# DeltaNet: the second half's inverse of the diagonal squares on GpSimd instead of VectorE

## The chip, the cores and the metric

The kernel runs on one core of a Trainium2 chip. A core has a matrix engine (PE, TensorE), a vector engine (DVE, VectorE), a scalar engine (ACT, ScalarE), a general engine (POOL, GpSimd) and a queue engine (SP, SyncE) that here only issues transfers. Each engine takes its own instructions in the order in which they were written and they meet through semaphores. ACT also issues transfers (rows "ACTq"): while it issues one it does nothing else.

The metric is the device time of one execution in microseconds (us). A profiled execution has a time of its own; all rows below are from it.

## The reference, cut to what matters

One layer of a hybrid encoder over 1024 tokens: four mixers feed a gated merge, then come cross attention and a mixture of experts. The change concerns the mixer called gated DeltaNet, run forward and backward over the sequence. Its core is one unit lower-triangular system for each chunk, head and direction:

```python
kk = jnp.einsum('bhntd,bhnsd->bhnts', kc, kc)
a_mat = jnp.where(strict, bc[..., None] * kk * decay, 0.0) + jnp.eye(c)
rhs = jnp.concatenate([vc * bc[..., None], kc * (bc * jnp.exp(gam))[..., None]], axis=-1)
sol = lax.linalg.triangular_solve(a_mat, rhs, left_side=True, lower=True, unit_diagonal=True)
u_val, k_cum = sol[..., :dv], sol[..., dv:]
# then chunk after chunk:
v_new = u_i - kc_i @ state
o = qd_i @ state + qk_i @ v_new
state = cd_i * state + kd_i^T @ v_new
```

## The kernel before, in words

**One list of steps.** `plan_schedule` writes one list of steps for all engines; each engine walks it and emits what it has to do for each step, so the list fixes the order on every engine. `dense(...)` lays out the matrix products of the weight panels (PE line L794) in parts; a `None` in the list given as `between` takes the next part (6 matmuls for most) and a named step stands between the parts. So PE works through panels, and the mixer's small products stand between their parts.

**DeltaNet in tiles.** The sequence is cut into TT = 8 tiles of 128 tokens; tile step i handles tile i forward and tile 7-i backward, for 4 heads: 8 matrices of 128x128 in each step. `gdn_a` (i = 0 to 7) builds the matrices and writes them to HBM (`gdn_out`), and ACT copies their 32x32 diagonal squares into `GDIAG` (L1728). After tile 3 and after tile 7 the squares of four tiles go to HBM (`gdn_ship`, L1767; halves b = 0 and 1), and `gdn_read` (L1777) brings them back so that each of the 128 partitions holds one square of 32x32 in `NUT[b]` and `NU[b]`.

**The inverse.** `gdn_inv(b, first, next)` inverts the 128 squares of half b at once, column by column: for j = 1 to 30 a product of a column with a row into a scratch tile (L2407) and a subtraction from the rows below (L2410), each of (31-j)*j elements in a partition and each waiting for the one ahead. A copy of half the partitions, turned, stands in front (L2402); two passes over 1024 elements (L2413, L2415) and two memsets (L2418) stand at the end. All of it is on DVE, in ten pieces of three columns that stand between other steps: those of half 0 from tile 5 of `gdn_a` on, those of half 1 within tiles 0 to 2 of `gdn_c`.

**Back and out.** `gdn_back(b)` (ACT, L1783) writes the inverses to HBM, `gdn_load_inv(i)` (ACT, L1803) loads those of one tile step into `XZC`, and `gdn_c(i, part)` with parts 0 to 6 solves and advances the state. In part 0 POOL spreads the squares into block-diagonal matrices `NX` and `NZ_` (L2825, four instructions in a step), which PE waits for with its first small product of the tile (L1015). In part 1 POOL makes two scaled copies of k for each direction (L2843, L2845). Half 1's inverses are first wanted for tile 4.

## Time and profile before

| what | us |
|---|---|
| median of 3 runs | 2041.04 (2040.8 to 2041.76) |
| the profiled execution | 2028.88 |
| its span | 2027.1 |
| PE busy in the span | 1878.2 (93%) |
| DVE busy | 1384.4 (68%) |
| ACT busy | 1078.0 (53%) |
| POOL busy | 308.8 (15%) |
| DeltaNet's `gdn_a` and both inverses, roughly | 668 to 844 |
| tile steps 0 to 7 of `gdn_c` | 773 to 945 |

Busy shares are means over stages that differ. What counts for the change is who waits for whom between 740 and 860 us, and what each engine does there. The profiled execution is 12.2 us shorter than the median of the timed runs.

### The profile page before, as it was taken

To read this page: it belongs to the slowest core of one execution; us is meant where nothing else is said; L and a number is where in the kernel's file an instruction comes from. 1 tells how busy PE (TensorE), PEld (TensorE's weight loads), DVE (VectorE), ACT (ScalarE), POOL (GpSimd) and SP (SyncE) were. 2 spreads that over 40 slices of the span, in tenths; PEclk is the share of its full clock that TensorE was granted. 3 is DMA by queue.
4 is the path that set the end of the run, shared out by engine and by line. 5 is a ranking of instruction groups with operands and counts; after the bars stand their busy time and mean duration, and the time that the engine had idled before them with its cause. 6 is when DMAs were issued, how large, how long until landed. Compare 5 with 4: busy or idle time off the path is not lost.

```text
span 2027.1 us, 32760 instructions
## 1 busy us (share of the span) xinstructions
PE 1878.2 (93%) x12949; PEld 1117.6 (55%) x12949; DVE 1384.4 (68%) x1833; ACT 1078.0 (53%) x1568; POOL 308.8 (15%) x269
## 2 busy tenths in 40 slices
PE   6999999999999989899999999995899999999991
PEld 3464565655544545677488755684455444444440
DVE  5555533799974797544733745437799999999997
ACT  4573223566646541223433533334588888888873
POOL 5000100344310512231000000000000111111103
PEclk9999999999999999999999999997899999999996
DMA  5411111212011562441522510404799999999986
GB/s 193 159 52 43 32 42 48 73 48 58 22 28 47 194 201 79 142 122 45 213 65 67 157 32 16 169 32 161 279 422 422 422 422 422 422 422 423 422 346 269
DMA packets 145817, 366.80 MB, mean 181 GB/s; under 512 B 39296, under 2 KB 94880, under 8 KB 119072
## 3 DMA queue, kind: packets, MB, share of 16 engines
q1 hardware_dynamic: 96608, 279.57, 36.3%
q10 hardware_dynamic: 40240, 52.50, 7.7%
q0 software_dynamic: 8848, 33.03, 4.2%
q8 instruction: 86, 1.41, 0.3%
q14 instruction: 35, 0.29, 0.0%
HBM read 314.14 MB, written 46.73 MB: 178 GB/s over the span
## 4 chain that ended last, share of the span: by engine, by line
PE 77%; DVE 10%; ACT 5%; issue 4%; DMA 2%; ACTq 1%; SPq 1%; DVEq 0%; POOLq 0%
PE psum L794 39%; PE psum L1185 24%; ACT arena L1631 2%; PE psum L1174 1%; PE psum L1109 1%; PE psum L1084 1%; DVE arena L2308 1%; PE psum L924 1%; PE psum L1203 1%; PE psum L811 1%; DMA gdn_lq<-arena 1%; PE psum L1066 1%; PE psum L1044 1%; DMA arena<-in_w_in_dram 1%; PE psum L935 1%
## 5 line engine op out<-in xcount | busy, mean ns | idle before, releaser
L794 PE MATMUL psum<-arena 128*128 128x512 f16 (+2 forms) x6000 | 1013.4, 326 | 17.6 <-ACT arena L1375 6.8
L794 PEld LDWEIGHTS psum<-arena 128*128 128x128 f16 x6000 | 567.6, 98 | 398.6 <-issue 15.6
L1185 PE MATMUL psum<-arena 128*128 128x512 f16 x2304 | 512.3, 381 | 14.7 <-issue 11.7
L751 DVE SCALAR_TENSOR_TENSOR arena<-arena 128x2048 f16<-128x2048 f32 x192 | 437.3, 2286 | 58.0 <-ACT arena L745 57.8
L745 ACT ACTIVATE arena<-arena 128x2048 f16<-128x2048 f32 x192 | 365.3, 1908 | 72.4 <-DMA arena<-in_w_dram 43.2
L1185 PEld LDWEIGHTS psum<-arena 128*128 128x128 f16 x2304 | 224.5, 98 | 280.4 <-issue 22.1
L1965 DVE SCALAR_TENSOR_TENSOR arena<-arena 128x512 f16<-128x512 f32 (+1 forms) x185 | 125.8, 699 | 114.0 <-ACT arena L1349 113.5
L2862 POOL DMA_INDIRECT arena<-xhat,arena x32 | 66.2, 2069 | 839.8 <-PE psum L1174 445.2
L1349 ACT ACTIVATE arena<-arena 128x512 f16<-128x512 f32 (+1 forms) x212 | 127.2, 616 | 51.5 <-issue 19.9
L1375 ACT ACTIVATE arena<-psum,arena 128x512 f32<-128x512 f32 x60 | 41.0, 684 | 140.3 <-PE psum L794 139.6
L1438 ACT ACTIVATE arena<-psum 128x512 f32<-128x512 f32 (+3 forms) x51 | 29.9, 586 | 126.4 <-PE psum L794 126.4
L1403 ACT ACTIVATE arena<-arena 128x256 f32<-128x256 f32 x64 | 26.7, 416 | 109.7 <-DVE arena L2000 108.6
L2757 POOL TENSOR_SCALAR arena<-arena 128x512 f32<-128x512 f32 x27 | 57.5, 2130 | 138.3 <-ACT arena L1349 138.3
L2293 DVE CUSTOM_DVE_ANT_0 arena<-psum,arena 128x1024 f32<-128x1024 f32 x64 | 75.6, 1219 | 2.3 <-PE psum L911 2.2
L1631 ACT ACTIVATE arena<-arena 128x1024 f32<-128x1024 f32 x64 | 72.9, 1147 | 7.3 <-DVE arena L2293 7.2
L1988 DVE SCALAR_TENSOR_TENSOR arena<-arena,psum 128x512 f32<-128x512 f32 x64 | 43.8, 684 | 42.7 <-PE psum L794 31.9
L2000 DVE SCALAR_TENSOR_TENSOR arena<-psum,arena 128x512 f32<-128x512 f32 x32 | 22.1, 690 | 65.1 <-PE psum L794 65.1
L2018 DVE SCALAR_TENSOR_TENSOR arena<-psum,arena 128x512 f16<-128x512 f32 x36 | 24.8, 690 | 59.9 <-ACT arena L1438 31.0
L1640 ACT ACTIVATE arena<-psum 128x512 f16<-128x512 f32 x64 | 34.7, 594 | 55.1 <-PE psum L924 34.3
L2825 POOL TENSOR_TENSOR arena<-arena 128x512 f32<-128x512 f32 x32 | 34.5, 1109 | 144.5 <-PE psum L1052 92.4
L1880 ACT ACTIVATE arena<-psum 128x512 f32<-128x512 f32 x64 | 38.2, 597 | 13.9 <-PE psum L1185 13.1
L1174 PE MATMUL psum<-arena 128*128 128x128 f32 x256 | 34.5, 279 | 8.8 <-DMA arena<-xhat,arena 8.8
(388 smaller groups left out, 2017.4 us busy)
## 6 DMA issues: line engine op xcount, KB each, us to landing
arena<-in_w_dram SPq DMA_DIRECT2D x192, 1024.0 KB, 11.9
arena<-in_merge_w_dram SPq DMA_DIRECT2D x64, 256.0 KB, 3.2
yrows<-arena ACTq DMA_DIRECT2D x32, 512.0 KB, 7.8
arena<-in_w_in_dram SPq DMA_DIRECT2D x48, 256.0 KB, 2.8
gdn_lq<-arena ACTq DMA_DIRECT2D x8, 1024.0 KB, 4.5
arena<-gdn_lq ACTq DMA_DIRECT2D x8, 1024.0 KB, 5.0
arena<-in_xattn_wkv_dram SPq DMA_DIRECT2D x32, 256.0 KB, 3.0
yrows<-arena POOLq DMA_DIRECT2D x1, 7680.0 KB, 24.1
```

What stands on the lines that cost most here:

```text
L745: nc.scalar.activation(half_of(pieces(e, m)[0], half), half_of(XLAND[m], half), ACT.Copy, scale=WS).then_inc(w_hi[m], 1)
L751: nc.vector.scalar_tensor_tensor(half_of(lo, half), half_of(XLAND[m], half), WS, half_of(hi, half), ALU.mult, ALU.subtract).then_inc(w_lo[ ...
L794: mm = nc.tensor.matmul(bank[prt[0]:prt[1], c0:c1], lhs[a](k), rhs[b](k), start=(k == 0 and a + b == 0), stop=(k == nk - 1 and a == 1))
L1174: tr = nc.tensor.transpose(PS[:, k // 4, (k % 4) * P:(k % 4) * P + P], xs[:, k, :], ident)
L1185: mm = nc.tensor.matmul(PS[:, bank, :], left[a][:, k, :], right[b][:, k, columns], start=k + a + b == 0, stop=(k == n - 1 and a == 1))
L1349: S.activation(W[i % 2][0][:, 2 * j:2 * j + 2, 0:wide], LAND[c % NLAND][:, :, 0:wide], ACT.Copy, scale=WS).then_inc(*act_hi.mark(c))
L1631: S.activation(DS[u % 2][:, m, :], DS[u % 2][:, m, :], ACT.Exp, scale=-1.0, bias=d_mx[u % 2][:, m:m + 1], accum_out=d_l[u % 2][:, m:m + 1])\
L1965: V.scalar_tensor_tensor(W[i % 2][1][:, 2 * j:2 * j + 2, 0:wide], LAND[c % NLAND][:, :, 0:wide], WS, W[i % 2][0][:, 2 * j:2 * j + 2, 0:wid ...
L1988: V.scalar_tensor_tensor(dst, gate, 1.0, bank, ALU.add, ALU.mult).then_inc(*e.mark(n))
L2293: V.tensor_tensor_reduce(out=DS[u % 2][:, m, :], in0=PS[:, 2 + 2 * m:4 + 2 * m, :].rearrange("p a b -> p (a b)"), in1=DWH[:, 896 - P * qt: ...
L2757: G.tensor_scalar(landed_c, landed_c, WS, None, ALU.mult).then_inc(*counter("pool_w_scaled").mark(chunk))
L2862: G.indirect_dma_start(XR[e % 2], None, XH_D, bass.IndirectOffsetOnAxis(IDX[:, e:e + 1], 0)).then_inc(rows_in[e % 2], 16)
```

## The change

Half 1's inverse moves from DVE to POOL as one step of all 30 columns. It stands in the list right behind piece 6 of half 0's inverse (columns 19 to 21), with `gdn_read(1)` ahead of it, which stood behind the two `gdn_load_inv` before. The scratch tile is `NX[0]` instead of `n_tmp`. `gdn_back(1)` moves from tile 3 to tile 1 of `gdn_c` and waits for POOL.

```diff
     for p in range(5, 10):
         gdn += inv(0, p) + [None] * (2 + (p < 8)) + [("gdn_load", p - 5)] * (p < 7)
-    gdn += [("gdn_back", 0)] + [None] * 6 + [("gdn_load_inv", 0), ("gdn_load_inv", 1), ("gdn_read", 1)] + [None] * 7
+        gdn += [("gdn_read", 1), ("gdn_inv", 1, 1, 31)] * (p == 6)
+    gdn += [("gdn_back", 0)] + [None] * 6 + [("gdn_load_inv", 0), ("gdn_load_inv", 1)] + [None] * 7
     for i in range(TT):
         for part in range(7):
-            gdn += [("gdn_back", 1)] * ((i, part) == (3, 1))
+            gdn += [("gdn_back", 1)] * ((i, part) == (1, 3))
             gdn += [("gdn_c", i, part)] + [None] * (1 + (i < 3 and part in (1, 4) and (i, part) != (2, 1)))
-            if i < 3 and part in (1, 2, 4) or (i, part) == (0, 5):
-                gdn += inv(1, 3 * i + (i > 0) + (1, 2, 4, 5).index(part))
...
-                    act.wait_ge(*counter("vec_gdn").at("inv", b))
+                    act.wait_ge(*counter("pool_gdn" if b else "vec_gdn").at("inv", b))
...
-                elif what == "gdn_inv":
+                elif what == "gdn_inv" and not step[1]:
...
+                elif what == "gdn_inv" and step[1]:
+                    b, first_row, next_row = step[1:]
+                    po = counter("pool_gdn")
+                    U, UT = NU[b], NUT[b]
+                    if first_row == 1:
+                        pool.wait_ge(diag_in[b], 32)
+                        pool.wait_ge(*counter("act_gdn").at("dt", TT - 1, 1))
+                        G.tensor_copy(U[0:64], UT[0:64].rearrange("p r c -> p c r")).then_inc(*po.mark("forward", b))
+                        pool.wait_ge(*po.last())
+                    for j in range(first_row, next_row):
+                        n = 31 - j
+                        part = NX[0].rearrange("p h n -> p (h n)")[:, 0:n * j].rearrange("p (r c) -> p r c", c=j)
+                        G.tensor_tensor(part, bc(U[:, j + 1:32, j:j + 1], P, n, j), bc(U[:, j:j + 1, 0:j], P, n, j), ALU.mult)\
+                            .then_inc(*po.mark("term", b, j))
+                        pool.wait_ge(*po.last())
+                        G.tensor_tensor(U[:, j + 1:32, 0:j], U[:, j + 1:32, 0:j], part, ALU.subtract).then_inc(*po.mark("row", b, j))
+                        pool.wait_ge(*po.last())
+                    if next_row == 31:
+                        G.tensor_scalar(UT, U.rearrange("p r c -> p c r"), -1.0, None, ALU.mult).then_inc(*po.mark("turned", b))
+                        pool.wait_ge(*po.last())
+                        G.tensor_scalar(U, U, -1.0, None, ALU.mult).then_inc(*po.mark("negative", b))
+                        pool.wait_ge(*po.last())
+                        for m in (U, UT):
+                            G.memset(m.rearrange("p r c -> p (r c)")[:, ::33], 1.0).then_inc(*po.mark(*(("inv", b) if m is UT else ("one", b))))
```

POOL before, from its last instruction of `gdn_a` (AFFINE_SELECT) to the first of `gdn_c` tile 0 (L2825, the spread):

```order
L2813 TENSOR_TENSOR arena<-arena 128x512
L2816 AFFINE_SELECT arena<-arena 128x512
L2825 TENSOR_TENSOR arena<-arena 128x512 x4
L2843 TENSOR_TENSOR arena<-arena 128x256
L2845 TENSOR_TENSOR arena<-arena 128x256
```

POOL after, at the end of the inverse and the start of `gdn_c` tile 0 (the spread is now L2848):

```order
L2829 TENSOR_TENSOR arena<-arena 128x30
L2832 TENSOR_TENSOR arena<-arena 128x30
L2835 TENSOR_SCALAR arena<-arena 128x1024
L2837 TENSOR_SCALAR arena<-arena 128x1024
L2840 MEMSET arena 128x32 x2
L2848 TENSOR_TENSOR arena<-arena 128x512 x4
L2866 TENSOR_TENSOR arena<-arena 128x256
```

The whole inverse, 65 instructions in all, stands on POOL ahead of tile 0's spread. ACT before, from the second load of `gdn_lq` to the read of half 1's squares (L1777):

```order
L1793 DMA arena<-gdn_lq 128x2048
L1375 ACTIVATE arena<-psum,arena 128x512
L1349 ACTIVATE arena<-arena 128x512 x2
L1375 ACTIVATE arena<-psum,arena 128x512
L1783 DMA gdn_inv<-arena 128x1024 x2
L1375 ACTIVATE arena<-psum,arena 128x512
L1803 DMA arena<-gdn_inv 128x4x32 x8
L1777 DMA arena<-gdn_diag 64x1024 x2
```

ACT after, the same place (the read is now L1776, the evacuation of a gate L1374):

```order
L1792 DMA arena<-gdn_lq 128x2048
L1776 DMA arena<-gdn_diag 64x1024 x2
L1374 ACTIVATE arena<-psum,arena 128x512
L1348 ACTIVATE arena<-arena 128x512 x2
L1374 ACTIVATE arena<-psum,arena 128x512
L1782 DMA gdn_inv<-arena 128x1024 x2
L1374 ACTIVATE arena<-psum,arena 128x512
L1802 DMA arena<-gdn_inv 128x4x32 x8
```

The read moved ahead of two evacuations and of `gdn_back(0)`. On DVE the 65 instructions of half 1's inverse are gone; PE's order is the same as before.

## Rows read from the trace of the kernel before

**Rows 1.** The page's part 1: busy us (share of the span) xinstructions.
```profile
PE 1878.2 (93%) x12949; PEld 1117.6 (55%) x12949; DVE 1384.4 (68%) x1833; ACT 1078.0 (53%) x1568; POOL 308.8 (15%) x269
```

**Rows 2.** Timeline of PE: start, us, engine line, operands xcount [idle before <-releaser].
```profile
745.28 28.67 PE L794 MATMUL psum<-arena 128*128 128x512 f16 x126 [6.14 <-DVE arena L1988]
776.30 2.76 PE L794 MATMUL psum<-arena 128*128 128x512 f16 x12 [2.35 <-ACT arena L1375]
778.99 0.60 PE L1015 MATMUL psum<-arena 32*32 32x32 f32 x32
...
804.50 0.34 PE L1024 MATMUL psum<-arena 32*32 32x32 f32 x5 [0.95 <-DVE arena L2428]
```

**Rows 3.** Waits of PE between 740 and 880 us: us in total, times, longest.
```profile
PE psum L1038 <- ACT arena L1751: 5.2, 3, 2.2
```

**Rows 4.** Timeline of POOL around the start of `gdn_c`.
```profile
720.42 0.63 POOL L2816 TENSOR_SCALAR_AFFINE_SELECT arena<-arena 128x512 f32<-128x512 f32 x1
773.20 4.48 POOL L2825 TENSOR_TENSOR arena<-arena 128x512 f32<-128x512 f32 x4 [52.15 <-DMA arena<-gdn_inv]
```

**Rows 5.** Timeline of ACT; ACTq rows are transfers that it issues.
```profile
742.75 0.38 ACTq L1767 DMA_DIRECT2D gdn_diag<-arena  x1
...
748.11 0.33 ACTq L1793 DMA_DIRECT2D arena<-gdn_lq  x1
...
763.93 0.82 ACTq L1783 DMA_DIRECT2D gdn_inv<-arena  x2
...
768.65 5.07 ACTq L1803 DMA_DIRECT2D arena<-gdn_inv  x8
773.83 1.10 ACTq L1777 DMA_DIRECT2D arena<-gdn_diag  x2
```

**Rows 6.** DVE, 600 to 1050 us, by line (both inverses): xcount | busy, mean ns.
```profile
L2410 DVE TENSOR_TENSOR arena<-arena 128x30 f32<-128x30 f32 (+14 forms) x60 | 19.9, 332 | 2.1
L2407 DVE TENSOR_TENSOR arena<-arena 128x30 f32<-128x30 f32 (+14 forms) x60 | 19.8, 330 | 1.6
```

**Rows 7.** Timeline of DVE: the end of half 0's inverse.
```profile
763.82 0.09 DVE L2418 MEMSET arena<- 128x32 f32 x1
```

**Rows 8.** Timeline of POOL: what its instructions take at several sizes.
```profile
38.10 1.49 POOL L2757 TENSOR_SCALAR arena<-arena 128x512 f32<-128x512 f32 x1 [3.72 <-ACT arena L1349]
122.39 2.35 POOL L2778 TENSOR_TENSOR arena<-arena 128x1024 f32<-128x1024 f32 x1 [13.13 <-ACT arena L1534]
257.28 1.27 POOL L2783 TENSOR_TENSOR arena<-arena 128x512 f32<-128x512 f32 x1 [2.10 <-DVE arena L2222]
668.50 1.04 POOL L2813 TENSOR_TENSOR arena<-arena 128x512 f32<-128x512 f32 x1 [80.58 <-DMA arena<-gdn_rows]
669.69 0.89 POOL L2816 TENSOR_SCALAR_AFFINE_SELECT arena<-arena 128x512 f32<-128x512 f32 x1 [0.15 <-POOL arena L2813]
...
847.89 0.61 POOL L2843 TENSOR_TENSOR arena<-arena 128x256 f32<-128x256 f32 x1 [0.67 <-DVE arena L2451]
864.80 4.03 POOL L2825 TENSOR_TENSOR arena<-arena 128x512 f32<-128x512 f32 x4 [13.96 <-PE psum L1052]
```

**Rows 9.** Timelines of POOL and DVE: the same operations beside each other and alone.
```profile
700.61 1.47 POOL L2813 TENSOR_TENSOR arena<-arena 128x512 f32<-128x512 f32 x1
...
700.07 1.11 DVE L2387 TENSOR_TENSOR arena<-arena 128x512 f32<-128x512 f32 x1
...
727.42 0.68 DVE L2387 TENSOR_TENSOR arena<-arena 128x512 f32<-128x512 f32 x1
```

**Rows 10.** DMA issues, 690 to 870 us: xcount, KB each, median us to landing.
```profile
gdn_diag<-arena ACTq DMA_DIRECT2D x2, 512.0 KB, 6.6
...
arena<-gdn_diag ACTq DMA_DIRECT2D x4, 256.0 KB, 5.0
```

**Rows 11.** Stretches of 2 us: length, busy (x) of PE, PEld, DVE, ACT, POOL, then PEclk.
```profile
746.00:748.00 2.00, 2.00 (x6) 0.76 (x5) 1.90 (x5) 0.00 (x0) 0.00 (x0) 0.51 1.43 206
748.00:750.00 2.00, 2.00 (x11) 0.88 (x9) 1.90 (x5) 0.63 (x1) 0.00 (x0) 1.00 1.13 242
```

## The prediction, made before the changed kernel was run

> **What bounds the kernel now.** First the shares: PE is busy for 93% of the span, DVE for 68%, POOL for 15% [rows 1]. That says that PE's waits are what costs, not DVE's load, but it is a mean. So next comes the timeline of PE from 740 us on, where DeltaNet's second stage begins. From 745.28 PE runs 126 panel matmuls without a gap, waits 2.35 us for ACT's evacuation of a gate, runs 12 more, and at 778.99 takes the first small product of tile 0 (L1015) [rows 2]. Behind that it waits little: 0.95 us for a DVE step at 804.50 [rows 2] and 5.2 us in three waits for ACT at L1038 [rows 3]. So in the stretch in which DVE makes half 1's inverse (about 786 to 844 us), DVE holds PE up once, for 0.95 us. The other three waits come behind transfers that ACT issues there and which stay.
>
> Then POOL's timeline: it ends `gdn_a` at 721.05, sits idle for 52.15 us until the inverses of half 0 are loaded, and starts tile 0's spread at 773.20 [rows 4]. This spread is on PE's way: L1015 reads its results. Before, POOL is ready 1.3 us ahead of PE (773.20 + 4.48 = 777.68 against 778.99). That is all the slack there is once POOL has more to do.
>
> **The change, part by part.** *When the inverse can start.* Half 1's squares are shipped at 742.75, and such a transfer lands after 6.6 us [rows 5, 10]: 749.35. `gdn_read(1)` stands behind the load that ACT issues at 748.11, so ACT waits about 1 us, issues two reads in 1.10 us [rows 5], and they land 5.0 us after issue [rows 10]. POOL starts at about 749.35 + 1.10 + 5.0 = 755.5. The read's bounds, from a landing of 3 to one of 7 us, make that 753.5 to 757.5. ACT's next instruction was due only later, so this wait costs nothing.
>
> *How long it takes on POOL.* An instruction with one spread-out operand takes 0.61 us for 256 elements and 1.04 for 512 [rows 8]: 1.68 ns an element and 0.18 us fixed. One with two full operands takes 1.27 us for 512 and 2.35 for 1024: 2.11 ns an element and 0.19 us fixed [rows 8]. The sum of (31-j)*j over 30 columns is 4960 elements. The 30 products have spread operands: 30 x 0.18 + 4960 x 0.00168 = 13.7 us. The 30 subtractions have full ones: 30 x 0.19 + 4960 x 0.00211 = 16.2 us. Each waits for the one ahead, and such a wait shows as 0.15 us between two POOL instructions [rows 8]: 60 x 0.15 = 9.0. Together 38.9 us. The turned copy of 1024 elements lies between the price of a select (0.89 us for 512, so 1.8) and that of a scaling (1.49 for 512, so 2.8) [rows 8]; I take 2.0, the copy being the simpler. The two scalings of 1024 elements cost 2.8 each at that rate, and memsets and waits 0.6: 6.2. Contention: from 755.5 to the end of DVE's half 0 at 763.9 [rows 7] both work on SBUF without a pause. Where they did before, a POOL instruction took 1.47 instead of 1.04 us and a DVE one 1.11 instead of 0.68 [rows 9]. POOL's part of that, over a stretch that itself grows to about 10 us, is 3.0. Sum: 2.0 + 38.9 + 6.2 + 3.0 = 50.1 us, so POOL is done at 805.6.
>
> *What that delays.* The spread of tile 0 was written behind the inverse on POOL, and it can't pass it. It takes 4.0 us with DVE idle [rows 8], so it ends at 809.6; L1015 then needs 0.4 us for the second direction and ends at 810.0, where before it ended at 779.59 [rows 2]. PE has no other work in its order to put there: the panel parts ahead of L1015 are used up by 779. The delay of **30.4 us** is a stall of PE. Nothing later takes it back, since PE is close to continuously busy in the tiles behind it and the later stages start from PE's progress.
>
> *What the stall hides.* DVE's half 0 ends some 3.5 us later from the contention, so its inverses arrive later and ACT's evacuation too; and the read is no longer in ACT's queue at 773.83 (1.10 us) [rows 5]. Both only move the moment at which PE begins to wait for POOL: 0. If POOL were in time they would cost 3.5 and give 1.1.
>
> *The clock.* After PE's wait of 6.14 us it ran at 0.51 of full speed (1.2 GHz) until 748, six matmuls in 2 us instead of 11, then at 1.00 [rows 2, 11]. That was 2.7 us at the low level, so 1.4 us lost. A wait of 30 us should do at least that: **+1.4**.
>
> *What leaves DVE.* Half 1's inverse is half of 19.9 + 19.8 us [rows 6] and some 5 us of passes. It lies beside PE's work, and what PE gets from it is the one wait of 0.95 us: **-0.95**. The bound above is the whole of L1038's waits too, -6.2; I stay with the low end because ACT's transfers end those.
>
> *`gdn_back(1)` moved.* It puts 0.82 us of issue [rows 5] in front of the ACT step for which PE waits at L1038 in tile 1; where it stood before PE didn't wait: **+0.8**, between 0 and 0.8.
>
> Sum: 30.4 + 1.4 - 0.95 + 0.8 = 31.7 us. The profiled execution would go from 2028.9 to 2060.6. The timed median stands 12.2 us above it, and I add the same 31.7 to the median: 2072.7.
>
> *Two rules of the Trainium skill.* The rows of POOL with one spread-out operand give 1.68 ns an element [rows 8], and they are not strided. The Trainium skill, GPSIMD Engine Reference, section 7, says that a read whose step is over 8 bytes costs about half as much again per element. The columns (128 bytes from row to row) and the two turned passes read that way; by that rule the sum would be some 7 us more. The same page, section 4.1, advises against elementwise work with two inputs on GpSimd, as about twice as slow as VectorE; DVE's mean here is 331 ns [rows 6], which would make 60 instructions 39 us before their waits instead of 29.9, and the sum 9 us more.
>
> **Rivals.** *A, the forecast:* POOL late by about 30 us, 2072.7.
>
> *B, POOL late by clearly more.* Short rows and strided reads have no row of before. If every element costs what the scaling does, (1.49 - 0.18)/512 = 2.56 ns [rows 8], the 60 instructions take 10.8 + 25.4 + 9.0 = 45.2 us instead of 38.9, and with passes at half as much again (+4) the sum grows by 10: 2083. For it: the two operands of the product and the turned views. Against it: 330 ns on DVE for a mean of 165 elements shows no penalty for short rows there.
>
> *C, POOL late by clearly less.* All elements at 1.68 ns, no gap between instructions, copy and scalings at the price of the select: 10.8 + 16.7 + 5.5 = 33 us, no contention, an early start at 753.5. POOL is done at 786.5 and the delay is 11 us plus the clock: 2053.5. Against it: the gap of 0.15 is a row.
>
> *D, not slower: GpSimd keeps up.* From 755.5 to 773.2 there are 17.7 us. If the inverse took less than that, PE would wait for nothing new, the read's 1.10 us and the 0.95 us would be gained, and if a free DVE also shortened the three waits of 5.2 us, the time would be 2041.04 - 7.2 = 2034. It decides at a mean of 0.25 us for each of the 60, gap included; the shortest arithmetic row on POOL is 0.61 us, and 60 fixed parts of 0.18 alone are 10.8. Nothing in the trace speaks for it.
>
> *E, the change doesn't begin where it says.* If the squares land late, after the end of half 0 at 764, there is no contention (-3) but a start 8.5 us later: 2078.
>
> **How the numbers follow.** A has 0.62, B 0.18, C 0.08, D 0.05, E 0.07. The range has to reach B and E and most of the way to C: 2057 to 2092. A difference of 0.2% (4.1 us) is about what a measurement of this kernel can tell from no change. D holds faster (0.03) and same (0.02), and the rest is slower; with a little for a surprise in the order, faster 0.03, same 0.03, slower 0.94.
>
> **What would show it.** In the changed profile: POOL's first inverse instruction at about 755; the last near 806; each of the 60 at 0.25 to 0.7 us with 0.15 between; PE idle for about 30 us ahead of L1015, with POOL as the releaser; PEclk near 0.5 for some 3 us after; DVE's last columns of half 0 stretched by a third or more; no wait at L1024 in tile 1. I am wrong if PE's wait there is short, if the wait ends with another engine, or if the time lost at L1015 is given back before 945 us.

## The result, and the profile after

The changed kernel takes 2083.02 us (median of 4 runs, 2079.7 to 2088.89) against 2040.92 for the kernel before on the same chip: a ratio of 1.0205, 95% interval 1.0174 to 1.0236, or 42.1 us more. The forecast was 31.7 us more. The profiled execution takes 2083.99 us (span 2082.2). The profile's part 1, after:

```profile
PE 1883.2 (90%) x12949; PEld 1118.9 (54%) x12949; DVE 1361.5 (65%) x1768; ACT 1077.8 (52%) x1568; POOL 348.9 (17%) x334
```

Against [rows 1], POOL has 65 instructions and 40.1 us more, DVE 65 instructions and 22.9 us less. None of these shares says that 42 us were lost; the timeline of PE does (start, us, line, xcount, [idle before <- releaser]), to be held against [rows 2]:

```profile
768.60 7.94 PE L793 MATMUL psum<-arena 128*128 128x512 f16 x36 [0.76 <-DVE arena L1987]
778.53 2.76 PE L793 MATMUL psum<-arena 128*128 128x512 f16 x12 [1.99 <-ACT arena L1374]
810.26 0.64 PE L1014 MATMUL psum<-arena 32*32 32x32 f32 x16 [28.96 <-POOL arena L2848]
812.26 0.64 PE L1014 MATMUL psum<-arena 32*32 32x32 f32 x16 [1.36 <-POOL arena L2848]
...
851.14 1.09 PE L1037 MATMUL psum<-arena 128*64 128x128 f32 x16 [3.69 <-ACT arena L1750]
```

PE sits idle for 28.96 us ahead of tile 0's first small product and 1.36 us more for the second direction, and POOL's spread (L2848) ends both. This is the wait that the prediction named. The last line is one that it made too small: in tile 1 PE waits 3.69 us for ACT, where it waited 0.96 before (at 813.97). POOL, for the same stretch, against [rows 4]:

```profile
761.15 1.96 POOL L2824 COPY arena<-arena 64x1024 f32<-64x1024 f32 x1 [38.88 <-DMA arena<-gdn_diag]
763.20 0.25 POOL L2829 TENSOR_TENSOR arena<-arena 128x30 f32<-128x30 f32 x1
...
765.51 1.06 POOL L2829 TENSOR_TENSOR arena<-arena 128x108 f32<-128x108 f32 x1
...
784.16 0.61 POOL L2829 TENSOR_TENSOR arena<-arena 128x240 f32<-128x240 f32 x1
784.86 0.69 POOL L2832 TENSOR_TENSOR arena<-arena 128x240 f32<-128x240 f32 x1
...
798.23 0.37 POOL L2829 TENSOR_TENSOR arena<-arena 128x108 f32<-128x108 f32 x1
...
801.39 3.63 POOL L2835 TENSOR_SCALAR arena<-arena 128x1024 f32<-128x1024 f32 x1
805.10 2.77 POOL L2837 TENSOR_SCALAR arena<-arena 128x1024 f32<-128x1024 f32 x1
807.93 0.22 POOL L2840 MEMSET arena<- 128x32 f32 x2
808.08 4.04 POOL L2848 TENSOR_TENSOR arena<-arena 128x512 f32<-128x512 f32 x4
```

The inverse runs without a break from 761.15 to 808.08, and the spread starts the moment it ends. It began 5.7 us later than forecast (4.5 us once PE's own restart, 1.2 us later in this profile, is taken off): the row of the copy says that it waited for the DMA that reads `gdn_diag`.

To add up, I take the distance from PE's restart after the wait of 6.14 us (745.28 before, 746.48 after) to the first L1015 (L1014) of tile 4: 126.8 us before, 166.3 after, so **39.5 us** arise between the two. The rows at the far end, before and after:

```profile
872.10 0.60 PE L1015 MATMUL psum<-arena 32*32 32x32 f32 x32
```

```profile
912.79 0.60 PE L1014 MATMUL psum<-arena 32*32 32x32 f32 x32
```

The two profiled spans differ by more than the timed medians, by 55.1 us: 1.2 ahead of the restart, 39.5 in this distance, 1.1 less from there to PE's last expert matmul, and 15.5 behind it. I call the time from the start of that matmul (L1185) to the end of the span the last phase: 39.6 us before, 55.0 after. VectorE's first sum there, L2703, in the timeline of before:

```profile
1994.26 9.86 DVE L2703 SCALAR_TENSOR_TENSOR arena<-arena 128x1024 f32<-128x1024 f32 x8 [9.05 <-issue]
```

And in the timeline of the changed kernel:

```profile
2049.85 9.65 DVE L2702 SCALAR_TENSOR_TENSOR arena<-arena 128x1024 f32<-128x1024 f32 x8 [25.01 <-issue]
```

The wait ends with "issue": no semaphore, the engine's own sequencer. What stands there is a loop of 15 passes over extra blocks (`beyond`, L754 to L760), whose body is skipped in each pass. The experiments below take the stall and this loop apart.

### The profile page after: what moved, and what is told of

Read it like the earlier page. It is cut to its first block, busy times and chain, and to the rows that moved or that the text cites. A ratio compares the mean times of both kernels' runs of the same rounds, so it can differ in the third digit from the quotient of the medians.

```text
span 2082.2 us, 32754 instructions
## 1 busy us (share of the span) xinstructions
PE 1883.2 (90%) x12949; PEld 1118.9 (54%) x12949; DVE 1361.5 (65%) x1768; ACT 1077.8 (52%) x1568; POOL 348.9 (17%) x334
## 4 chain that ended last, share of the span: by engine, by line
PE 75%; DVE 8%; ACT 5%; issue 5%; DMA 3%; POOL 2%; ACTq 1%; DVEq 1%; SPq 1%; POOLq 0%
PE psum L793 38%; PE psum L1184 24%; ACT arena L1630 2%; PE psum L1173 1%; PE psum L1083 1%; PE psum L1108 1%; DVE arena L2307 1%; PE psum L923 1%; POOL arena L2832 1%; POOL arena L2829 1%; PE psum L1202 1%; PE psum L810 1%; PE psum L1065 1%; PE psum L1043 1%; DMA gdn_lq<-arena 1%
## 5 line engine op out<-in xcount | busy, mean ns | idle before, releaser
L793 PEld LDWEIGHTS psum<-arena 128*128 128x128 f16 x6000 | 568.9, 99 | 405.0 <-issue 24.7
L1374 ACT ACTIVATE arena<-psum,arena 128x512 f32<-128x512 f32 x60 | 41.0, 684 | 176.2 <-PE psum L793 175.4
L1437 ACT ACTIVATE arena<-psum 128x512 f32<-128x512 f32 (+3 forms) x51 | 29.9, 586 | 127.9 <-PE psum L793 127.9
L1639 ACT ACTIVATE arena<-psum 128x512 f16<-128x512 f32 x64 | 34.7, 595 | 55.1 <-PE psum L923 34.3
L2848 POOL TENSOR_TENSOR arena<-arena 128x512 f32<-128x512 f32 x32 | 33.6, 1082 | 102.1 <-PE psum L1051 102.1
```

The source lines that it names most:

```text
L793: mm = nc.tensor.matmul(bank[prt[0]:prt[1], c0:c1], lhs[a](k), rhs[b](k), start=(k == 0 and a + b == 0), stop=(k == nk - 1 and a == 1))
```

## The experiments

Every kernel was timed against the kernel before on its own chip (experiments 1 to 4 on one, 5 to 8 on a second, 9 to 12 on a third); ratios are to that. "Stretch" is the distance from PE's restart to the first L1015 of tile 4, against the 126.8 us of the kernel before.

**1. The inverse left out (none).** The kernel leaves out half 1's inverse (the turned copy, the columns and both passes) and keeps everything else of the change, the wait for the reads and the two memsets among it.

```diff
-                        G.tensor_copy(U[0:64], UT[0:64].rearrange("p r c -> p c r")).then_inc(*po.mark("forward", b))
...
-                    for j in range(first_row, next_row):
+                    for j in ():
...
-                        G.tensor_scalar(UT, U.rearrange("p r c -> p c r"), -1.0, None, ALU.mult).then_inc(*po.mark("turned", b))
...
-                        G.tensor_scalar(U, U, -1.0, None, ALU.mult).then_inc(*po.mark("negative", b))
```

> The changed kernel with half 1's inverse left out on POOL except the two memsets (the squares of half 1 are not inverted): POOL is free for tile 0's spread. Theory (PE waits because the spread stands behind the inverse on POOL): PE's wait of 28.96 us at tile 0's first small product goes to 0, the 40 us that the change cost go with it, and what stays is the moved write-back; time within 2037 to 2045 against 2041 before. Rival (the loss comes from GpSimd sharing SBUF with VectorE and from the read of the squares that was moved into other transfers, and the clock that falls): with the read still early, at least 5 us of the loss stay, 2047 or more.

Measured: 2048.53 us, ratio 1.0038 (1.0022 to 1.0053). PE's wait at the first L1015 is 0.17 us, the stretch 131.4 (+4.5). So the stall is POOL's work and nothing else. But the time misses the range of 2037 to 2045 and lies where the rival's number was (2047 or more), and not by the rival's cause: in tile 1 PE waits 3.42 us at L1038 and then runs 16 matmuls in 1.98 instead of 1.09 us, which is the moved write-back (experiment 3), and the rest of the 8.2 us over the kernel before is in none of the stages up to the last phase.

**2. Half the columns (cols15).** Columns 16 to 30 are left out, 2480 of 4960 elements.

```diff
-                    for j in range(first_row, next_row):
+                    for j in range(first_row, 16):
```

> The changed kernel with columns 16 to 30 of half 1's inverse left out on POOL (half 1 is not fully inverted). In the changed kernel's trace these 30 instructions take 17.2 us (784.2 to 801.4). Theory: POOL's time is PE's wait one for one, so the wait of 28.96 us becomes 11.8 and the time 2083 - 17 = 2066. Rival (the wait is set by something else, such as the landing of the inverses of half 0, about 777): the wait falls to 0 or stays near 29.

Measured: 2062.67 us, ratio 1.0108 (1.0085 to 1.0131); PE waits 11.14 + 1.36 us, stretch 147.6 (+20.7). In the changed kernel these columns take 17.2 us on POOL, and PE's wait shrank by 17.8. Microsecond for microsecond, what POOL works there, PE waits.

**3. The write-back at tile 3 again (backlate).**

```diff
-            gdn += [("gdn_back", 1)] * ((i, part) == (1, 3))
+            gdn += [("gdn_back", 1)] * ((i, part) == (3, 1))
```

> The changed kernel with the write-back of half 1's inverses at tile 3 again. The wait of 29 us stays. Theory: the write-back in tile 1 cost 2.78 us of issue on ACT instead of the 0.8 foreseen, made PE's wait at L1037 3.69 us instead of 0.96 and let the clock fall behind it; with it back at tile 3 that wait is about 1 us, no stretch at half clock follows, and the time is 3 to 6 us lower, 2077 to 2080. Rival (the clock falls in tiles 1 and 2 as an after-effect of the long wait): half-clock stretches stay there and the time moves by 2 us or less.

Measured: 2077.37 us, ratio 1.0191 (1.0169 to 1.0213), stretch 159.0 (+32.2). The wait at L1038 in tile 1 is 0.87 us again. The stretch is 7.3 us shorter than in the changed kernel. Of these 1.4 are from a shorter stall (27.25 us), and 1.0 arises between the first small products of tiles 0 and 1 (26.1 us against 27.1), ahead of the write-back, because the clock came back sooner behind the stall. The distance from tile 1 to tile 4 is 75.4 us in the changed kernel and 70.5 here, so the move costs **4.9 us**, not 0.8. The ratios differ by 0.0014 and their intervals overlap, so the timing alone wouldn't show it. ACT in the changed kernel tells why (ACTq rows are issues):

```profile
845.63 2.22 ACTq L1802 DMA_DIRECT2D arena<-gdn_inv  x4
847.89 2.78 ACTq L1782 DMA_DIRECT2D gdn_inv<-arena  x2
850.71 0.78 ACT L1750 ACTIVATE arena<-psum 64x256 f32<-64x256 f32 x2 [6.31 <-issue]
```

The two issues took 2.78 us behind four others, where they took 0.82 in [rows 5], and PE waited for all of it. (What stands ahead of the prediction, that ACT does nothing else while it issues, is too strong: in the kernel before an ACTIVATE runs from 748.05 to 748.68 beside the issue at 748.11. What waits is the instruction written behind the issues, as here.) Then the clock fell, and the next panel products took 4.45 instead of 2.76 us:

```profile
852.17 4.45 PE L793 MATMUL psum<-arena 128*128 128x512 f16 x12
```

Stretches of 2 us of the changed kernel (PE, PEld, DVE, ACT, POOL busy, then PEclk, DMA share, GB/s):

```profile
816.00:818.00 2.00, 2.00 (x45) 1.16 (x38) 1.45 (x6) 0.00 (x0) 0.00 (x0) 0.50 0.00 0
818.00:820.00 2.00, 2.00 (x10) 0.84 (x8) 0.87 (x2) 0.69 (x1) 0.00 (x0) 0.91 0.03 11
...
852.00:854.00 2.00, 2.00 (x12) 0.67 (x6) 1.36 (x3) 1.32 (x4) 0.00 (x0) 0.62 0.75 293
854.00:856.00 2.00, 2.00 (x6) 0.76 (x5) 0.00 (x0) 0.00 (x0) 0.00 (x0) 0.52 0.44 127
```

The first two rows are the restart after the long stall: half speed (1.2 GHz) up to about 818, some 8 us after PE took up work at 810.26, its wait of 1.36 us included. The last two are after the wait of 3.69 us: half speed again. It fell once more at 876, after a wait of 2.49. That last fall isn't the write-back's: in backlate too the 16 matmuls of tile 2's L1038 take 1.92 us behind a wait of 2.08, and experiment 5 shows the like in the kernel before.

**4. In four pieces (pieces).** Columns 1 to 7 where the change has them, the rest behind tiles 0, 1 and 2 of `gdn_c`; scratch in another buffer; write-back at tile 3.

```diff
-        gdn += [("gdn_read", 1), ("gdn_inv", 1, 1, 31)] * (p == 6)
+        gdn += [("gdn_read", 1), ("gdn_inv", 1, 1, 8)] * (p == 6)
...
+            gdn += {(0, 1): [("gdn_inv", 1, 8, 16)], (1, 1): [("gdn_inv", 1, 16, 25)], (2, 1): [("gdn_inv", 1, 25, 31)]}.get((i, part), [])
```

> Half 1's inverse on POOL in four pieces that fit between its other steps: columns 1 to 7 where the change puts the whole, 8 to 15 behind tile 0's copies of k, 16 to 24 behind tile 1's, 25 to 30 and the passes behind tile 2's; write-back at tile 3. Scratch in an idle tile. Theory: the amount of work on POOL is harmless (47 us in 15 us gaps), only its place hurts; the wait at tile 0's first product is under 3 us and the time is 2038 to 2043, the same as before. The other terms: sharing SBUF with VectorE's half 0 costs PE about 1 to 2 us ahead of tile 0, the vanished wait at L1024 gives 0.95. Rival (GpSimd is too slow for this work anywhere): spreads of tiles 1 to 3 come late, PE waits 5 us or more in each, 2055 or more.

Measured: stretch 126.9 (+0.1), wait for POOL 0.29 us. So at the same pace the same work costs the stretch nothing where no needed step waits behind it; in the changed kernel pace and place cost together, as cols15 shows, where less work in the same place cost less. (The write-back's 4.9 us are undone here too.) But the timing says 2047.23 us, ratio 1.003 (1.002 to 1.0041): above the range of 2038 to 2043, and 6.9 us slower with an undisturbed stretch. PE's last expert matmul starts 0.2 us later than before, relative to the restart. The loss lies behind it.

**5. The kernel before once more (control).** No edit.

> The kernel before, unchanged, run as if it were a new one. Its one profile so far ends 12 us under the median of its timed runs, and its last phase (from the last expert instruction L1185 of PE to the end of the span) takes 39.6 us, where all five changed kernels show about 55; DVE L2703 waits 9.1 us there in it and 24.7 to 25.0 in the others. Theory 1 (the tail is the same in every kernel, and the profile of before was an exception): the last phase is again about 55 us here, the profiled span is near 2040, and the timed median is within 0.1% of the kernel before. Rival (the changes lengthen the tail by 15 us): 40 us again, a span near 2027. If theory 1 holds, the timed difference of a kernel is to be compared with the stretch from 745 us to the last L1185, and the tail leaves the sum.

Measured: 2036.66 us, ratio 1.0002 (0.9992 to 1.0012), span 2033.1; the last phase takes 44.6 us and VectorE waits 13.9 us in the loop. Neither 40 nor 55: both my theories were too simple. The last phase of the first profile was 5 us shorter than this one, and the changed kernels are some 10 us above this one. The stretch is 128.3 us here; the clock fell after a wait of 2.00 us in tile 2, as it hadn't in the first profile. In readearly and before_skip below, which have the same inverses on VectorE, the stretch is 128.6 and 128.4. So stretches are good to some 2 us, and 126.8 is the shortest of the four: against the other three the changed kernel's is about 38 us longer.

**6. Four pieces, none beside VectorE's half 0 (pieces_wait).**

```diff
                         pool.wait_ge(diag_in[b], 32)
+                        pool.wait_ge(*counter("vec_gdn").at("inv", 0))
```

> The kernel with the inverse on GpSimd in four pieces between the tiles, and in addition GpSimd's first instruction waits for the end of VectorE's half 0, so that the two never work on SBUF together there. Theory 1 (working beside GpSimd stretches VectorE, 1.99 us for a copy that takes 0.27 alone, and this costs PE 1.65 us at L1988 and 1.62 at L1374): half 0 ends at about 764, these two waits go back to 0 and to 2.35 in the place where before has it, and the stretch from PE's restart at 745 to tile 4's L1015 is 125 to 126.8 us, so 0.5 to 2 us less than with pieces alone; time 2039 to 2045. Rival (the waits come from the reads' transfers, which share the DMA engines with the load of gdn_lq): the waits stay, the stretch stays at about 127, and the time is 2044 to 2048. Second rival (GpSimd pieces now end later and stall tile 1 or 2): a new wait for POOL at L1015 in tiles 1 to 3, the stretch over 128.

Measured: 2045.43 us, ratio 1.0045 (1.0031 to 1.006), stretch 127.6. Half 0 ends at 764.85, and PE runs its 126 matmuls without the wait of 1.65 us at L1988 that pieces has; the same 108-element subtraction takes 0.27 us. So the sharing of SBUF did cost PE that wait. The rest of theory 1 didn't come: PE's wait for ACT's evacuation is 1.60 us and not 2.35, 0.9 us come back as a wait for POOL's spread, the stretch is above its range of 125 to 126.8, and the time doesn't fall. VectorE in the changed kernel, beside POOL's turned copy:

```profile
760.95 0.27 DVE L2406 TENSOR_TENSOR arena<-arena 128x108 f32<-128x108 f32 x1
761.26 1.99 DVE L2409 TENSOR_TENSOR arena<-arena 128x108 f32<-128x108 f32 x1
763.28 0.27 DVE L2406 TENSOR_TENSOR arena<-arena 128x84 f32<-128x84 f32 x1
```

**7. Only the read moved (readearly).** Both inverses stay on VectorE.

```diff
-        gdn += inv(0, p) + [None] * (2 + (p < 8)) + [("gdn_load", p - 5)] * (p < 7)
+        gdn += inv(0, p) + [None] * (2 + (p < 8)) + [("gdn_load", p - 5)] * (p < 7) + [("gdn_read", 1)] * (p == 6)
...
-("gdn_load_inv", 1), ("gdn_read", 1)]
+("gdn_load_inv", 1)]
```

> The kernel before with only the read of half 1's squares moved forward, to where the change has it; both inverses stay on VectorE. It measures by itself how long the read takes to land when it is issued right behind the load of gdn_lq: 5.0 us by the prediction, 9.2 to 9.9 by the profile of the changed kernel. Theory 1 (the transfers share the DMA engines, whatever GpSimd does): 9 to 10 us for the reads and for the load of gdn_lq here too. Rival (the late start came from something else, GpSimd's own wait or its start): about 5 us. In both, ACT has 1.1 us less to issue at 773.8, the stretch from 745 to tile 4's L1015 is 125.5 to 126.8 us, and the time is 2037 to 2042, so within 0.2% of before.

Measured: 2036.82 us, ratio 0.9998 (0.9988 to 1.0009). PE's wait for ACT's evacuation ahead of tile 0 is 1.16 us instead of 2.35, but the stretch is 128.6 and not 125.5 to 126.8: in tile 2 PE waits 3.12 us at L1038 and then runs 16 matmuls in 1.98. The DMA issues from 745 to 765 us (xcount, KB each, median us to landing):

```profile
arena<-gdn_lq ACTq DMA_DIRECT2D x2, 1024.0 KB, 9.1
...
arena<-gdn_diag ACTq DMA_DIRECT2D x2, 256.0 KB, 8.8
```

The read lands after 8.8 us without any work on POOL; in the changed kernel after 9.2, where from 755 to 760 us the DMA share is 1.04. In [rows 10] the median of four such reads is 5.0. So the late start isn't GpSimd's doing. That it is the load of `gdn_lq`, issued just ahead of the read, fits these rows; but the DMA engines weren't idle around the read of the kernel before either (a share of 0.82 from 773 to 780 us), and no run moves the read away from that load alone.

**8. The whole block behind tile 0 (behind0).** One step of 30 columns, behind the spread and the scaled copies of tile 0.

```diff
-        gdn += [("gdn_read", 1), ("gdn_inv", 1, 1, 31)] * (p == 6)
+        gdn += [("gdn_read", 1)] * (p == 6)
...
+            gdn += [("gdn_inv", 1, 1, 31)] * ((i, part) == (0, 1))
```

> The whole inverse in one step on GpSimd as in the change, but written behind tile 0's spread and its copies of k, with the read still early; the write-back stands at tile 3, the scratch tile is another. Theory 1 (what costs is where a block of 47 us stands in GpSimd's order, and any tile's spread behind it stalls PE by what is left of it): no wait for POOL in tile 0; the block starts at about 780 to 783 and ends at 824 to 828, the spread of tile 1 follows at 829 to 832 and takes 4 us, so PE waits for POOL at L1015 of tile 1, due in before 21 us after tile 0's (at about 801); a stall of about 28 to 32 us, time 2069 to 2076. Rival (the cost is the late start or the sharing with VectorE in half 0): the stall is clearly under 20 us, time 2045 to 2060. Theory 1 also expects no instruction of VectorE above 0.5 us in half 0's last columns.

Measured: 2077.61 us, ratio 1.0194 (1.0174 to 1.0213). The stall has moved one tile on:

```profile
782.29 0.81 PE L1015 MATMUL psum<-arena 32*32 32x32 f32 x32
...
831.86 0.64 PE L1015 MATMUL psum<-arena 32*32 32x32 f32 x16 [26.73 <-POOL arena L2849]
833.85 0.64 PE L1015 MATMUL psum<-arena 32*32 32x32 f32 x16 [1.35 <-POOL arena L2849]
```

The block takes 44.6 us (785.19 to 829.75) where half 0 isn't beside it, 2.3 less than in the changed kernel. Tile 1's L1015 comes 28.5 us later than before, relative to the restart. The stretch is 158.0 us (+31.2). Theory 1 holds for the stall of 28 to 32 us. The time isn't in its range of 2069 to 2076, and on a chip where the kernel before takes 2036.57 it is 41.0 us more; the loop (23.0 us of wait here) is the one stage outside the stretch that is seen to be longer.

**9 to 12. The loop at the end.** In these profiles VectorE waits in the loop as follows. Four kernels whose VectorE has as many instructions ahead of it as before: 9.05 (before), 13.9 (control), 15.2 (readearly), and 9.04 in pad below. Seven with 65 fewer: 24.7 to 25.0 (changed, none, cols15, backlate, pieces), 24.4 (pieces_wait), 23.0 (behind0). Pieces_wait's chain of waits has both parts of it (start, us, what):

```profile
1989.13 0.26 issue
1989.88 0.27 issue
1990.64 0.26 issue
...
2001.66 0.70 DVEq L757
2002.38 0.71 DVEq L757
2003.09 0.70 issue
```

At first a pass takes 0.75 us; then each single instruction of a pass takes 0.70. In before, a pass has two pieces of 0.27 us (1988.30, 1988.57), so 0.53 us. *pad* is pieces_wait with 65 memsets of one column on VectorE, where half 1's columns had stood:

```diff
+                elif what == "gdn_pad":
+                    for k in range(step[3] + (step[1:3] == (0, 4))):
+                        V.memset(n_tmp[:, 0:1], 0.0).then_inc(*v.mark("pad", *step[1:3], k))
+                        dve.wait_ge(*v.last())
```

> The kernel with the inverse in four pieces behind VectorE's, plus 65 memsets of one column on DVE in the ten places where half 1's columns stood, so that DVE has as many instructions ahead of the loop over extra blocks as in the kernel before. Theory 1 (where DVE's code lies sets how fast the loop's passes go: with 65 fewer instructions a pass takes 0.75 us where it took 0.53, and more passes fall into the stretch where every step takes 0.70): passes at 0.53 us again, the wait ahead of DVE L2703 back from 24.4 to 9 to 15 us, span 2033 to 2036, time 2036 to 2040, so within 0.2% of before. Rival (it comes from GpSimd's instructions or the order on ACT): the wait stays at 23 to 25 us and the time at 2044 to 2047. The stretch from 745 to tile 4's L1015 stays at 127 to 128 us in both.

*before_skip*, *after_skip* and *pieces_skip* are the kernel before, the changed one and pieces_wait with one condition around the loop:

```diff
-            with eng.Fori(0, NOV) as j:
-                with eng.If(number > j):
-                    body(j + NE, j)
+            with eng.If(number > 0):
+                with eng.Fori(0, NOV) as j:
+                    with eng.If(number > j):
+                        body(j + NE, j)
```

> The kernel before, with the loop over extra blocks (15 passes, each of which finds nothing to do) wrapped in one more condition, so that PE, DVE, ACT and SP step over it in one branch. Theory 1 (between the last expert and the final sums an engine spends 8 to 25 us in these passes: steps of 0.27 us where they go fast, of 0.70 us where they go slowly, and the two profiles of the unchanged kernel differ by 6 us in it alone): DVE L2703 no longer waits behind 'issue' for 9 to 14 us, the last phase is bound by the gathered rows' landing instead and takes 38 to 40 us, span 2025 to 2028, time 2027 to 2031, so 6 to 10 us less than before. Rival (the passes lie beside the transfers and cost nothing): time within 4 us of before, with DVE waiting for a DMA just as long.

> The changed kernel with the same one condition around the loop over extra blocks. Theory 1 (the changed kernels carry some 10 us more in this loop, 24.4 to 25.0 us instead of 13.9 to 15.2, which has nothing to do with GpSimd's inverse): the time falls by 13 to 16 us, to 2066 to 2070, and its distance from the kernel before with the same condition is what the stretch from 745 us to the last L1185 shows, 38 to 40 us. Rival (the distance of 42 us is all from the inverse, and the tail differs by chance between profiles): it keeps a distance of 42 or more.

> The kernel with the inverse in four pieces behind VectorE's, with the one condition around the loop over extra blocks. It compares the move itself, without its stall and without the loop, with the kernel before under the same condition. Theory 1 (moved off the critical path the inverse on GpSimd is worth nothing to PE, since VectorE held PE up by 0.95 us only): within 2 us of the kernel before with the same condition, 2027 to 2032. Rival (a free VectorE shortens later waits): 3 to 6 us less than that.

Measured, the first four on one chip (before: 2033.31, 29 runs), the last on that of experiment 6 (before: 2036.57):

| kernel | us | ratio (95%) | last phase, us |
|---|---|---|---|
| pad | 2031.24 | 0.9994 (0.9981 to 1.0007) | 40.4 |
| before_skip | 2032.19 | 1.0002 (0.999 to 1.0013) | 40.3 |
| pieces_skip | 2032.61 | 0.9994 (0.9982 to 1.0007) | 40.3 |
| after_skip | 2072.16 | 1.0181 (1.0153 to 1.0209) | 39.0 |
| pieces_wait (exp. 6) | 2045.43 | 1.0045 (1.0031 to 1.006) | 54.5 |

The branches of the loop in pieces_wait, and then in pad (the line is L759 there): duration in ns min/median/max, first and last start.

```profile
L757 DVEq COMPARE_BRANCH  x15: 13/56/700, 1988.2 to 2010.8; - x15
```

```profile
L759 DVEq COMPARE_BRANCH  x15: 50/56/72, 1987.8 to 1995.3; - x15
```

Instructions that compute nothing bring the loop from 22.6 us back to 7.5, and the 0.45% are gone. One condition does the same. The Trainium skill, Runtime: NRT & Kernel Launch, section "Instruction fetch mechanics", says that a taken branch to a target outside the two blocks of instructions that an engine holds forces a fetch by DMA. That the place of the code matters agrees with it; that each pass fetches isn't shown, since from 1984 us on this trace has one or two packets on each instruction queue. What is shown is that 65 instructions more or less on VectorE ahead of the loop go with 0.53 or 0.75 us a pass in all eleven profiles; whether by the number, the address or the alignment of what follows isn't separated. What turns on the 0.70 us is open: it came only while the DMA engines were fully busy with gathered rows, on VectorE for five or more passes with the shorter code, for the last few only in control and readearly, and in before and pad not at all. Pad ran on another chip than pieces_wait, so how much of its gain comes from the pace of a pass and how much from a chip on which the 0.70 us didn't come isn't separated.

Three expectations failed here. before_skip isn't 6 to 10 us faster: with the loop at its fast pace, VectorE would only wait for the gathered rows instead:

```profile
1991.09 1.32 DVE L2704 SCALAR_TENSOR_TENSOR arena<-arena 128x1024 f32<-128x1024 f32 x1 [6.71 <-DMA arena<-yrows,arena]
```

The time of after_skip, 2072.16, is above its range of 2066 to 2070. And after_skip's distance from before_skip is 40.0 us by medians, as expected from the stretch (168.1 against 128.4), but the changed kernel's own was 42.1, so the loop seems to account for some 2 us of the *difference* and not for 10. This isn't settled: each has four timed runs, and the ratios, 1.0205 and 1.0181, have intervals that overlap, so that neither 0 nor 10 us is excluded. The profile of the kernel before, 2028.88 us, is also no guide to its timed runs on that chip (2037 to 2042) and isn't one of them; on the third chip 29 runs of the same kernel lie between 2028.1 and 2038.0. What the slower ones lose, and whether it is in the loop, isn't known. No version beats the kernel before by a measurable amount: pad, pieces_skip, readearly and before_skip are all within 0.2% of it.

## Why the prediction was right or wrong, by its own steps

**Right: what bounds.** PE waits ahead of L1015 with POOL as the releaser, by an instruction that stands behind the inverse; POOL's delay is PE's delay (experiments 1, 2, 4, 8). The direction and the range held, and the delay of L1015, the largest term, came within 2 us (32.1 against 30.4), in part by luck: POOL started 4.5 us later than forecast and took 3.2 us less.

The sum had 31.7 us, the stretch shows 39.5:

| term | forecast | measured |
|---|---|---|
| POOL's start, after PE's restart | 10.2 (at 755.5) | 14.7 (at 761.15) |
| the inverse on POOL | 50.1 | 46.9 |
| spread and second direction | 4.4 | 4.8 |
| so L1015 later by | 30.4 | 32.1 |
| the clock behind the stall | +1.4 | +2.5 |
| wait at L1024 gone | -0.95 | 0 |
| the write-back moved | +0.8 | +4.9 |
| sum | 31.7 | 39.5 |

The wait at L1024 is gone as forecast, but nothing of it is left at tile 4: from tile 1 to tile 4 backlate takes 70.5 us, and so does the kernel before. The clock fell in tile 2 of backlate and not in the profile of before, which is the chance that control shows.

**The start** was mis-sized by 4.5 us. I took the landing of the reads from rows of another stretch (5.0 us) with a bound of 7; it was 9.2, beside two loads of 1 MB. The bound came from nothing. The trace had what should have set it: in the DMA issues of 745 to 765 us, before, the loads of `gdn_lq` took 8.8 us. Rival E's mechanism, a late landing, came true for about half of its 8.5 us, without the end of the contention that it went with.

**The time on POOL** was close, and two errors cancelled within it. The 60 instructions have 33.5 us of busy time, 3.8 of it from working beside VectorE (an estimate: each size occurs twice, and this is the first occurrence less the second): 29.7 against 29.9. The contention was 3.8 against 3.0 by this reckoning, which takes in all of VectorE's work; in behind0, where half 0 is over, the 60 have 31.0 us, so 2.5 come from half 0 itself. The gaps were 0.08 us and not 0.15: 4.6 in all and not 9.0. The wait of 0.15 in [rows 8] stood behind an instruction of 512 elements; I had one row. The passes took 6.7 against 6.2. So rival B's mechanism (more for each element) is refuted, although its 2083 is the measured time, which is chance: at 240 elements the rows above have 0.61 and 0.65 to 0.69 us, where B asks for 0.79.

**Strided reads and the factor of two.** The columns of 30 elements read four bytes of every 128 and took 0.25 us, at the prices of the unstrided rows; the scaling with the turned view took 3.63 against 2.77 us. So the step costs a third more in that one instruction, 0.9 us in all. The Trainium skill, GPSIMD Engine Reference, section 7, gives half as much again, and by it the sum had been 7 us more; here the measurement decides. The factor of two of the same page's section 4.1 would have given 39.7 us for the 60 instructions without their gaps (twice DVE's 19.85; the prediction wrote 39), where 29.7 was measured.

**The write-back** is the step whose mechanism failed. I priced it as its two issues alone. They went into a queue with other issues just ahead of the instruction that PE waits for (2.78 us, not 0.82), and a wait of 3.69 us costs more than itself, because PE comes back at half speed. I counted the clock once, for the large stall, where each of the smaller ones can cost it again.

**The clock** behind the stall: 2.5 us in the changed kernel and 1.5 in backlate, which has the same code up to there. The half speed lasted some 8 and 6 us from the moment when PE took up work again, and not 2.7.

**Hidden terms.** VectorE's half 0 ended 2.2 us later relative to the restart (3.5 forecast), and as said it moved only the start of PE's wait.

**What the prediction had no term for:** the loop at the end. No stage of DeltaNet is in it; by pad it follows the 65 instructions that VectorE no longer has ahead of it. Experiments 4 and 6 lose 6.9 and 8.9 us with an undisturbed stretch, and with the condition around the loop (pieces_skip) that loss is gone; its share in the 42.1 is open, as said. The profile of before had the row (9.05 us of "issue"), but nothing in it said that the row could change.

## What to carry to other kernels

Ask of work that moves to an idle engine what stands behind it in that engine's order, and who waits for that: here 47 us on an engine with 15% load cost 32, and the same work in four pieces cost nothing that the timing can tell once the loop was out of the way (pieces_skip, ratio 0.9994). Take a transfer's landing time from the stretch in which it will run, and price a transfer that you put on an engine's queue by who waits for the next instruction there. When a kernel's time moves and no stage between does, look at the waits that end with "issue": here they were sequencer time in a loop, and changed with the number of instructions ahead of it. And profile the unchanged kernel twice before you read 2 us out of a difference: here its second profile was 6 us longer.

## What the runs showed of the hardware that was not expected

- One VectorE subtraction of 108 elements took 1.99 us instead of 0.27 while POOL made a turned copy, where the earlier rows show 0.43 us more for an instruction of 0.68 [rows 9]. It ended at 763.25, 0.14 us after the copy (763.11). The other way round POOL's product of 108 elements took 1.06 us, from 765.51 to 766.57, beside a VectorE pass over 1024 elements that ended at 766.34. Both look like a wait for the whole instruction of the other engine; no run separates this.
- Short operands cost POOL nothing beyond size: 0.24 to 0.25 us for 30 elements, 0.18 us fixed plus 1.8 ns an element for the product, 0.19 plus 1.9 for the subtraction.
- The clock fell to 0.50 to 0.62 behind waits of 2 to 3.7 us, and of kernels with much the same wait at tile 2's L1038 some lost it (control, 2.00 us, then 1.79 us for 16 matmuls) and some didn't (before, 2.22 us, then 1.09).
- A skipped pass of a loop took 0.53 or 0.75 us on VectorE depending on the number of instructions ahead, and in one phase 0.70 us for every instruction of it.
